# Linear attention's seams: two weight splits issued later, and three turned groups behind an output tile instead of two

## The chip, the cores and the metric

The kernel runs on one core of a Trainium2 chip. The metric is the device time of one execution in microseconds (us). The kernel before has a median of 2364.84 us over 3 runs (2358.07 to 2365.14). All other times come from one profiled execution, whose own time is 2364.55 us and whose span from first to last instruction is 2362.6 us.

## The reference, cut to what matters

Two layers of a first block (a projection, a spatial gating group and an attention group, an output projection) are followed by one layer of gated linear attention and a convolutional feed-forward part, all on 1024 tokens of width 1024 in fp32. What the change touches:

```python
# end of each layer of the first block: y = [y_a, y_b], 1024 wide
out = jnp.einsum('bse,ed->bsd', y, w_out[l])

# linear attention, per chunk of 64 tokens (4 heads, dk 128, dv 256)
q_dec, k_inv = qi * jnp.exp(bi), ki * jnp.exp(-bi)
scores = jnp.where(causal, einsum('bhtd,bhsd->bhts', q_dec, k_inv), 0.0)
o = einsum('bhts,bhsv->bhtv', scores, vi) + einsum('bhtd,bhdv->bhtv', q_dec, state)
state = state * exp(b_last) + einsum('bhsd,bhsv->bhdv', ki * exp(b_last - bi), vi)
# its end
return (rms_norm(o) * jax.nn.silu(r)) @ w_out
```

## The kernel before, in words

Every large product is made of three fp32r matmuls: both operands are split into a high part (`hi`) and a low part (`lo`), and `three_products` (lines 200 to 202) adds hi*hi, hi*lo and lo*hi into one PSUM bank. Weights come in pieces of 128x2048 by DMA into `w_raw` (two slots). ScalarE (ACT) writes `w_hi` (`split_hi`, line 168), VectorE (DVE) writes `w_lo` (`split_lo`, line 184). Each engine has a program written out by hand; its instructions run in that order and wait on semaphores. A load of piece u waits until the piece that held its slot has been split. A piece's first split waits until the matmuls that used its `w_hi` slot are done.

The left operand needs tokens in the free dimension, so activations are turned by TensorE (PE) transposes. `TurnHalf` turns one half of the width in eight groups of four 128x128 transposes: `pe` (line 229) writes a PSUM bank, `act` (line 235) takes it to `hT_hi`, `dve` (line 239) subtracts to get `hT_lo`. With `banks` banks, group g waits until group g - banks is through `dve`.

An output projection runs by `pe_wide_tile`: a tile is 128 tokens by 512 columns, half of the depth, 12 matmuls. In its first pass over eight tiles the first four tiles use banks 0 to 3, and behind each of them two groups of the second half are turned, into banks 4 to 7. Ahead of tile 4, PE waits for all eight groups. There are three such passes: in `MixerOut.pe_first` (called in `mixer_to_mixer` and in `mixer_to_gla`) and in `gla_out_ffn`.

The linear attention has three programs in a row in one block. `mixer_to_gla` ends with four pieces of columns for the queries and keys; behind each piece v, ACT and DVE split piece v + 2, the last one being the second piece of the core's gate weights. `gla_core` then waits for the last scaled keys (`heads_done`). For each of eight tiles of 128 tokens, PE computes scores in two parts (lines 1793 and 1797), the second from the mixed keys `KM` that ACT makes (`key_map`, lines 1897 and 1899); GpSimd (POOL) makes `KE` (line 1779), PE turns it (line 1807), ACT takes it to `KEt` (line 1910), and PE multiplies it with the values (line 1815). DVE masks the scores (line 1946) and updates the state (line 1952 for the first tile). Behind the core's tiles come the gate's products, ACT's `gate` (line 1921) and DVE's `gated` (line 1989), and, one group behind each tile, the turning of the first half of the output's width. `gla_out_ffn` starts its first pass when all eight of those groups are through DVE.

Of the kernel before, what the change touches and what calls it, by code (L numbers as in the profile page):

```python
# [16 lines left out]
TT = SEQ // P  # L17
# [190 lines left out]
class TurnHalf:  # L208
# [9 lines left out]

    def bank(self, g):
        return self.p.ps[:, self.bank0 + g % self.banks, :]  # L220

    def place(self, hT, g):
        return hT[:, self.k0 + g // 2, g % 2 * 512:(g % 2 + 1) * 512]
# [856 lines left out]
class MixerOut:  # L1080
# [51 lines left out]
    def pe_first(self, pe):  # L1132

        w = self.w
        for t in range(TT):
            if t == 4:
                pe.wait_ge(self.turn.lo_done, self.turn.GROUPS)
            mm = pe_wide_tile(self.p, 0, t, t, w.slot(0))
            if t < 4:
                self.turn.pe(pe, 2 * t, self.src)  # L1140
                self.turn.pe(pe, 2 * t + 1, self.src)
        mm.then_inc(self.half_done, 1)
        w.ready(pe, 1)
        for t in range(TT):
            pe_wide_tile(self.p, 1, t, t, w.slot(1)).then_inc(self.acc_ready, 1)
        w.ready(pe, 2)
        for t in range(TT):
            pe.wait_ge(self.acc_free, t + 1)
            mm = pe_wide_tile(self.p, 0, t, t, w.slot(2))
        mm.then_inc(self.half_done, 1)  # L1150
# [185 lines left out]
GLA_PIECES = 8  # L1336
# [24 lines left out]
def mixer_to_gla(prog, a, outs, ins, follows, src, x_src, x_dst):  # L1361
# [28 lines left out]
    U0 = OUT_PIECES  # L1390
# [12 lines left out]
    w = Weights(prog, pieces + [(follows, u) for u in range(2)], used, resident=1)  # L1403
# [168 lines left out]
    def act_program(act):  # L1572
        def square(act, t):
            act.wait_ge(out.x_done, t + 1)
            norm.square(act, t, ring.tile(t))

        def take(g, t, bank):
            act.wait_ge(acc_ready, g * TT + t + 1)
            nc.scalar.activation(V[:, t, g * WIDE:(g + 1) * WIDE], prog.ps[:, bank, :], ACT.Copy,
                                 scale=norm.inv(t)).then_inc(acc_free, 1)  # L1580

        out.act_first(act)
        for i in range(TT + TURN):
            if i == 0:
                w.split_hi(act, 4)
            at_tile(out.act_tile, act, i)
            at_tile(nxt.hi, act, i - TURN)
            at_tile(square, act, i - 2)
            if i == TT:
                w.split_hi(act, 5)  # L1590
        norm.root(act, 0)
        norm.root(act, 1)
        act.wait_ge(norm.inverted, 2)
        for t in range(4):
            take(0, t, V_TILES[t])
        w.split_hi(act, U0 + 2)
        act.wait_ge(wa_landed, 16)
        nc.scalar.activation(wa[:, :, 0, :], wa_raw[:], ACT.Copy).then_inc(wa_hi_done, 1)
        for t in range(4, TT):
            take(0, t, V_TILES[t])  # L1600
        act.wait_ge(scales_ready, 1)
        for half in range(2):
            nc.scalar.activation(scales[:, half * 512:(half + 1) * 512], prog.ps[:, 4 + half, :],
                                 ACT.Copy).then_inc(scales_taken, 1)
        w.split_hi(act, U0 + 3)
        act.wait_ge(small_landed, SMALL)
        for n in range(2 * GH):
            h, half = n // 2, n % 2
            act.wait_ge(z_ready, n + 1)
            if n >= 2:  # L1610
                act.wait_ge(z_exp, n - 1)
            nc.scalar.activation(tmp[:, n % 2, :], prog.ps[:, 4 + n % 4, :], ACT.Abs,
                                 bias=ba[:, h:h + 1]).then_inc(z_abs, 1)
            act.wait_ge(z_abs, n + 1)
            nc.scalar.activation(B[:, h, half * 512:(half + 1) * 512], tmp[:, n % 2, :], ACT.Exp,
                                 scale=-1.0).then_inc(z_exp, 1)
        act.wait_ge(z_exp, 2 * GH)
        for h in range(GH):
            nc.scalar.activation(B[:, h, :], B[:, h, :], ACT.Ln, bias=1.0).then_inc(z_log, 1)
        w.split_hi(act, U0 + 4)  # L1620
        for t in range(TT):
            take(1, t, t)
        w.split_hi(act, U0 + 5)
        for h in range(GH):
            act.wait_ge(b_done, h + 1)
            nc.scalar.activation(Q[:, h, :], B[:, h, :], ACT.Exp, scale=1.0 / TAU).then_inc(e_done, 1)
        nc.scalar.activation(DEC[:], Bv[:, :, :, CH - 1], ACT.Exp, scale=1.0 / TAU).then_inc(e_done, 1)
        act.wait_ge(e_done, GH + 1)
        for h in range(GH):
            nc.scalar.activation(B[:, h, :], B[:, h, :], ACT.Exp, scale=-1.0 / TAU).then_inc(e_done, 1)  # L1630
        for v in range(4, GLA_PIECES):
            w.split_hi(act, U0 + v + 2)

    def dve_program(dve):
# [46 lines left out]
        for v in range(4, GLA_PIECES):  # L1681
            for i in range(4):
                h, half = (v % 2) * 2 + i // 2, i % 2
                tok = slice(half * 512, (half + 1) * 512)
                dve.wait_ge(acc_ready, 2 * TT + 4 * (v - 4) + i + 1)
                if v < 6:
                    dve.wait_ge(q_scaled, h + 1)
                    nc.vector.scalar_tensor_tensor(Q[:, h, tok], prog.ps[:, i, :], DK ** -0.5, Q[:, h, tok],
                                                   ALU.mult, ALU.mult).then_inc(acc_free, 1)
                else:  # L1690
                    dve.wait_ge(k_scaled, h + 1)
                    nc.vector.tensor_tensor(K[:, h, tok], prog.ps[:, i, :], B[:, h, tok],
                                            ALU.mult).then_inc(acc_free, 1)
            w.split_lo(dve, U0 + v + 2)
    def heads_done(engine, heads=GH):

        engine.wait_ge(acc_free, 2 * TT + 8 + 2 * heads)
# [4 lines left out]
def gla_core(prog, a, into, stream, follows):  # L1702

    nc = prog.nc
    _, w_in, Q, K, V, DEC, norm, heads_done, k_scaled, z_ready = into
# [24 lines left out]
    w = Weights(prog, [(stream, u) for u in range(NU)] + [(follows, u) for u in range(2)], used, prior=w_in)  # L1730
# [22 lines left out]
    turn = TurnHalf(prog, 0, 0, 6)  # L1753
# [126 lines left out]
    def act_program(act):  # L1880
# [11 lines left out]
        def key_map(t):  # L1892
            if t >= 2:
                act.wait_ge(s_ready, t - 1)
                act.wait_ge(ke_done, t - 1)
            for h in range(GH):
                nc.scalar.activation(KM[:, t % 2, h, 0:CH], K[:, h, t * P:t * P + CH], ACT.Copy,
                                     scale=DEC[:, h, 2 * t:2 * t + 1])
            nc.scalar.activation(KM[:, t % 2, :, CH:P], K[:, :, t * P + CH:(t + 1) * P], ACT.Copy
                                 ).then_inc(km_done, 1)  # L1900

        heads_done(act)
        key_map(0)
        key_map(1)
        for t in range(TT):
            if t + 1 < TT:
                act.wait_ge(ke_turned, t + 1)
                if t >= 2:
                    act.wait_ge(kv_ready, t - 1)
                nc.scalar.activation(KEt[:, t % 2, :, :], prog.ps[:, 1, :].rearrange("p (h d) -> p h d", h=GH),  # L1910
                                     ACT.Copy).then_inc(ke_taken, 1)
            if t + 2 < TT:
                key_map(t + 2)
            if t >= 1:
                head_squares(t - 1)
# [13 lines left out]
        for i in range(TT + 2):  # L1929
            if i < TT:  # L1930
                gate(TT + i)
            if i >= 2:
                turn.act(act, i - 2)
            if i == TT - 1:
                w.split_hi(act, 5)

    def dve_program(dve):
        dve.wait_ge(zeroed, 2)
# [3 lines left out]
        def mask_scores(t):  # L1942
            dve.wait_ge(s_ready, t + 1)
            if t >= 2:
                dve.wait_ge(inter, t - 1)
            nc.vector.copy_predicated(S[:, t % 2, :, :], mask[:].unsqueeze(1).to_broadcast([P, GH, P]),
                                      prog.ps[:, 0, :].rearrange("p (h d) -> p h d", h=GH)).then_inc(s_done, 1)
# [28 lines left out]
                                               ALU.mult).then_inc(o_done, 1)  # L1976

        mask_scores(0)
        for t in range(TT):
            if t + 1 < TT:  # L1980
                state(t)
                mask_scores(t + 1)
            if t >= 1:
                normed(t - 1)
# [13 lines left out]
        for i in range(TT + 2):  # L1998
            if i < TT:
                gated(TT + i)  # L2000
            if i >= 2:
                turn.dve(dve, i - 2)
            if i == TT - 1:
                w.split_lo(dve, 5)

    def src(t, k):
        return V[:, t, k * P:(k + 1) * P]
# [34 lines left out]
def gla_out_ffn(prog, a, core, outs, ups, downs, x_src, x_dst, y_dst):  # L2042
# [129 lines left out]
    def pe_program(pe):  # L2172
# [7 lines left out]
        for t in range(TT):  # L2180
            if t == 4:
                pe.wait_ge(turn.lo_done, turn.GROUPS)
            mm = pe_wide_tile(prog, 0, t, t, w.slot(0))
            if t < 4:
                turn.pe(pe, 2 * t, src)
                turn.pe(pe, 2 * t + 1, src)
        mm.then_inc(o_half_done, 1)
        w.ready(pe, 1)
        for t in range(TT):
# [370 lines left out]
```

## Time and profile before

| what | value |
|---|---|
| median of 3 runs | 2364.84 us (2358.07 to 2365.14) |
| profiled execution | 2364.55 us, span 2362.6 us |
| PE busy | 2298.8 us, 97% of the span |
| VectorE busy | 1064.9 us, 45% |
| ScalarE busy | 895.5 us, 38% |
| GpSimd busy | 271.2 us, 11% |
| mean granted clock of PE | 0.990 |

PE is nearly always busy, so the time can be read as PE's busy time plus what PE waits. A row of the waits names the instruction that waited, the one that released it, the sum of the idle time, how often, and the longest. The granted clock is 1.00 at 2.4 GHz and 0.50 at 1.2 GHz.

### The profile page before, as it was taken

The page shows a single profiled execution, that of the slowest core. Times are in us where ns is not written, and L with a number is a line of the kernel's source. Part 1 is how long each engine was busy: PE and PEld are TensorE (multiplying, and loading weights), DVE is VectorE, ACT ScalarE, POOL GpSimd, SP SyncE. Part 2 cuts the span into 40 slices and gives each one's busy share as a digit, 9 for nine tenths or more (in the row PEclk, how much of TensorE's full clock was granted, in tenths as well). Part 3 has the DMA queues.
Part 4 walks back from the last instruction along what each step waited for, and adds up shares of the span by engine and source line. Part 5 has one row for each costly group of instructions (what it writes and reads, how often), then busy time and mean ns, then how long its engine had stood idle before and what let it go on. Part 6 is the DMA issues. An engine that isn't in the chain of part 4 may idle for free.

```text
span 2362.6 us, 28595 instructions
## 1 busy us (share of the span) xinstructions
PE 2298.8 (97%) x11648; PEld 1930.4 (82%) x11648; DVE 1064.9 (45%) x1433; ACT 895.5 (38%) x1420; POOL 271.2 (11%) x276
## 2 busy tenths in 40 slices
PE   7999999989999999999999999999999999999998
PEld 7887788878988778888878888787888888888887
DVE  4323388844433258882614243325433433443343
ACT  5122477733321268772434042213221222222242
POOL 0097200000029600000003020000000000000000
PEclk9999999999999999999999999999999999999999
DMA  5111000032311000004311100133111111114332
GB/s 197 36 54 36 1 1 1 1 134 104 101 47 54 18 1 1 1 1 143 141 40 36 63 19 22 59 109 107 52 38 53 53 36 53 53 61 162 107 124 72
DMA packets 104050, 141.34 MB, mean 60 GB/s; under 512 B 11574, under 2 KB 64998, under 8 KB 103942
## 3 DMA queue, kind: packets, MB, share of 16 engines
q1 hardware_dynamic: 103942, 139.84, 17.9%
q8 instruction: 76, 1.25, 0.2%
q14 instruction: 32, 0.26, 0.0%
HBM read 123.05 MB, written 16.78 MB: 59 GB/s over the span
## 4 chain that ended last, share of the span: by engine, by line
PE 51%; DVE 2%; ACT 1%; issue 0%; POOL 0%; DVEq 0%; ACTq 0%
PE ps L200 16%; PE ps L202 16%; PE ps L201 16%; PE ps L1815 1%; PE ps L1828 1%; PE ps L1837 1%; DVE hT_lo L291 0%; PE ps L229 0%; PE ps L1500 0%; ACT w_hi L168 0%; DVE w_lo L184 0%; PE ps L1793 0%; PE ps L1797 0%; PE ps L276 0%; DVE OUT L2432 0%
## 5 line engine op out<-in xcount | busy, mean ns | idle before, releaser
L200 PE MATMUL ps<-w_hi,hT_hi 128*128 128x512 f32 (+1 forms) x1760 | 683.2, 388 | 16.7 <-DVE hT_lo L239 10.0
L202 PE MATMUL ps<-w_hi,hT_lo 128*128 128x512 f32 (+1 forms) x1760 | 675.9, 384 | 0.0
L201 PE MATMUL ps<-w_lo,hT_hi 128*128 128x512 f32 (+1 forms) x1760 | 675.6, 384 | 0.0
L184 DVE TENSOR_TENSOR w_lo<-w_raw,w_hi 128x2048 fp32r<-128x2048 f32 x90 | 207.8, 2309 | 547.6 <-ACT w_hi L168 545.1
L200 PEld LDWEIGHTS ps<-w_hi,hT_hi 128*128 128x128 f32 x1760 | 334.1, 190 | 84.1 <-issue 14.3
L202 PEld LDWEIGHTS ps<-w_hi,hT_lo 128*128 128x128 f32 x1760 | 333.7, 190 | 65.3
L201 PEld LDWEIGHTS ps<-w_lo,hT_hi 128*128 128x128 f32 x1760 | 334.4, 190 | 63.0 <-issue 0.5
L168 ACT ACTIVATE w_hi<-w_raw 128x2048 fp32r<-128x2048 f32 x72 | 137.7, 1913 | 522.2 <-PE ps L202 522.2
L200 PE MATMUL ps<-hT_hi,w_hi 128*128 128x512 f32 x832 | 325.9, 392 | 5.1 <-DVE X L2372 2.8
L201 PE MATMUL ps<-hT_lo,w_hi 128*128 128x512 f32 x832 | 325.4, 391 | 0.0
L202 PE MATMUL ps<-hT_hi,w_lo 128*128 128x512 f32 x832 | 325.4, 391 | 0.0
L200 PEld LDWEIGHTS ps<-hT_hi,w_hi 128*128 128x128 f32 x832 | 157.3, 189 | 38.2 <-issue 3.0
L201 PEld LDWEIGHTS ps<-hT_lo,w_hi 128*128 128x128 f32 x832 | 157.3, 189 | 32.9
L202 PEld LDWEIGHTS ps<-hT_hi,w_lo 128*128 128x128 f32 x832 | 157.2, 189 | 32.8
L1048 DVE TENSOR_REDUCE nmx<-ps 128x1 f32<-128x1024 f32 x128 | 155.7, 1218 | 59.5 <-PE ps L878 59.5
L1061 DVE TENSOR_TENSOR PT_lo<-ps,PT_hi 128x512 fp32r<-128x512 f32 x256 | 163.7, 681 | 1.1 <-ACT PT_hi L975 1.1
L975 ACT ACTIVATE PT_hi<-ps 128x512 fp32r<-128x512 f32 x256 | 139.2, 595 | 63.4 <-PE ps L890 59.1
L981 ACT ACTIVATE PR<-ps,nmx 128x1024 f32<-128x1024 f32 x128 | 142.9, 1116 | 15.0 <-DVE nmx L1048 13.9
L890 PEld LDWEIGHTS ps<-ident,PR 128*128 128x128 f32 x1024 | 114.9, 140 | 38.7 <-issue 21.8
L890 PE MATMUL ps<-ident,PR 128*128 128x128 f32 x1024 | 138.0, 276 | 6.8 <-DVE PT_lo L1061 5.2
L2409 DVE SCALAR_TENSOR_TENSOR A<-ps,CW,A 128x1023 f32 (+3 forms) x44 | 56.4, 1283 | 175.1 <-ACT A L2324 171.0
L904 PE MATMUL ps<-PT_hi,VS 128*128 128x256 f32 x512 | 130.4, 293 | 1.4 <-DVE PT_lo L1061 1.4
(191 smaller groups left out, 2367.3 us busy)
## 6 DMA issues: line engine op xcount, KB each, us to landing
w_raw<-in_w_in SPq DMA_DIRECT2D x22, 1024.0 KB, 5.1
w_raw<-in_ffn_w_up SPq DMA_DIRECT2D x44, 512.0 KB, 4.8
w_raw<-in_ffn_w_down SPq DMA_DIRECT2D x22, 1024.0 KB, 4.9
x_mid<-X SPq DMA_DIRECT2D x24, 512.0 KB, 2.8
w_raw<-in_gla_w_in SPq DMA_DIRECT2D x12, 1024.0 KB, 5.2
X<-in_x SPq DMA_DIRECT2D x16, 512.0 KB, 6.9
w_raw<-in_w_out SPq DMA_DIRECT2D x8, 1024.0 KB, 6.7
X<-x_mid SPq DMA_DIRECT2D x16, 512.0 KB, 7.3
```

The source lines that it names most:

```text
L168: self.p.nc.scalar.activation(self.p.w_hi[:, slot, 0:stream.size], self.p.w_raw[:, slot, 0:stream.size], ACT.Copy).then_inc(self.hi_ready, 1)
L184: engine.tensor_tensor(self.p.w_lo[:, slot, 0:size], self.p.w_raw[:, slot, 0:size], plane(self.p.w_hi[:, slot, 0:size]), ALU.subtract).the ...
L200: nc.tensor.matmul(out, a_hi, b_hi, start=first, stop=False)
L201: nc.tensor.matmul(out, a_hi, b_lo, start=False, stop=False)
L202: return nc.tensor.matmul(out, a_lo, b_hi, start=False, stop=last)
L890: mm = nc.tensor.transpose(prog.ps[:, 4 + half, j * P:(j + 1) * P], self.PR[m % 3][:, k * P:(k + 1) * P], prog.ident[:])
L904: nc.tensor.matmul(prog.ps[:, 7, 0:256], v, self.PT_hi[:, g % 2, k, :], start=(k == 0), stop=False)
L975: nc.scalar.activation(self.pt_of(self.PT_hi, m, half), self.bank_of(half), ACT.Copy).then_inc(self.pt_hi, 1)
L981: nc.scalar.activation(self.PR[n % 3][:].rearrange("p (a b) -> p a b", a=2), prog.ps[:, 2 * (n % 2):2 * (n % 2) + 2, :], ACT.Exp, bias=sel ...
L1048: nc.vector.tensor_reduce(self.nmx[:, n:n + 1], prog.ps[:, 2 * (n % 2):2 * (n % 2) + 2, :], AX.XY, ALU.max, negate=True).then_inc(self.max ...
L1061: nc.vector.tensor_tensor(self.pt_of(self.PT_lo, m, half), self.bank_of(half), plane(self.pt_of(self.PT_hi, m, half)), ALU.subtract).then_ ...
L2409: nc.vector.scalar_tensor_tensor(o, banks(j, part)[:, 0:SEQ - back].unsqueeze(1), CW[:, 2 - back, bass.ds(f, 1)], o, ALU.mult, ALU.add).th ...
```

## The change

There are three edits. The core's last weight split of `mixer_to_gla` is issued by `gla_core` instead: on ACT behind the mixed keys of tiles 0 and 1, on DVE behind the first masked scores. The split of the last piece of the core (the second of the output's weights) is issued behind the last turned groups, not ahead of them. In the three first passes three groups are turned behind tiles 0 and 1 and two behind tile 2, where two were turned behind each of tiles 0 to 3.

```diff
@@ TurnHalf
+    def behind(self, t):
+        return range(3 * t, min(3 * t + 3, self.GROUPS))
@@ MixerOut.pe_first, and the same in gla_out_ffn
-            if t < 4:
-                self.turn.pe(pe, 2 * t, self.src)
-                self.turn.pe(pe, 2 * t + 1, self.src)
+            for g in self.turn.behind(t):
+                self.turn.pe(pe, g, self.src)
@@ mixer_to_gla, act_program
-        for v in range(4, GLA_PIECES):
+        for v in range(4, GLA_PIECES - 1):
             w.split_hi(act, U0 + v + 2)
@@ mixer_to_gla, dve_program
-            w.split_lo(dve, U0 + v + 2)
+            if v < GLA_PIECES - 1:
+                w.split_lo(dve, U0 + v + 2)
@@ gla_core, act_program
         key_map(0)
         key_map(1)
+        w_in.split_hi(act, len(w_in.pieces) - 1)
@@ gla_core, act_program
             if i >= 2:
                 turn.act(act, i - 2)
-            if i == TT - 1:
-                w.split_hi(act, 5)
+        w.split_hi(act, 5)
@@ gla_core, dve_program
         mask_scores(0)
+        w_in.split_lo(dve, len(w_in.pieces) - 1)
@@ gla_core, dve_program
             if i >= 2:
                 turn.dve(dve, i - 2)
-            if i == TT - 1:
-                w.split_lo(dve, 5)
+        w.split_lo(dve, 5)
```

## Rows read from the trace of the kernel before

**Rows 1.** The page: the engines' busy time, and the chain that ended last.

```profile
PE 2298.8 (97%) x11648; PEld 1930.4 (82%) x11648; DVE 1064.9 (45%) x1433; ACT 895.5 (38%) x1420; POOL 271.2 (11%) x276
PE 51%; DVE 2%; ACT 1%; issue 0%; POOL 0%; DVEq 0%; ACTq 0%
```

**Rows 2.** Waits of PE, whole span: who waited for whom, us, times, longest.

```profile
PE ps L200 <- DVE hT_lo L239: 10.0, 4, 5.3
PE ps L1797 <- ACT KM L1899: 1.4, 1, 1.4
PE ps L1815 <- ACT KEt L1910: 0.7, 1, 0.7
```

**Rows 3.** Timeline of a first pass: start, us, engine, line, count, [idle before].

```profile
506.25 0.39 PE L202 MATMUL ps<-w_hi,hT_lo 128*128 128x512 f32 x1
...
508.53 1.04 PE L229 MATMUL ps<-ident,G 128*128 128x128 f32 x8
509.17 1.08 ACT L235 ACTIVATE hT_hi<-ps 128x512 fp32r<-128x512 f32 x2 [2.53 <-PE ps L229]
509.80 1.29 DVE L239 TENSOR_TENSOR hT_lo<-ps,hT_hi 128x512 fp32r<-128x512 f32 x2 [2.33 <-ACT hT_hi L235]
511.14 0.50 PE L200 MATMUL ps<-w_hi,hT_hi 128*128 128x512 f32 x1 [1.58 <-DVE hT_lo L239]
...
1530.09 1.03 PE L229 MATMUL ps<-ident,V 128*128 128x128 f32 x8
1533.71 1.04 PE L229 MATMUL ps<-ident,V 128*128 128x128 f32 x8
```

**Rows 4.** Timeline of the core's end, PE, ACT and DVE.

```profile
1515.19 1.47 PE L229 MATMUL ps<-ident,V 128*128 128x128 f32 x12
1515.97 0.59 ACT L235 ACTIVATE hT_hi<-ps 128x512 fp32r<-128x512 f32 x1
1516.45 1.91 ACT L168 ACTIVATE w_hi<-w_raw 128x2048 fp32r<-128x2048 f32 x1
1516.71 0.68 DVE L239 TENSOR_TENSOR hT_lo<-ps,hT_hi 128x512 fp32r<-128x512 f32 x1
1518.39 2.29 DVE L184 TENSOR_TENSOR w_lo<-w_raw,w_hi 128x2048 fp32r<-128x2048 f32 x1 [0.99 <-ACT w_hi L168]
1520.60 1.28 DVE L239 TENSOR_TENSOR hT_lo<-ps,hT_hi 128x512 fp32r<-128x512 f32 x2
1521.98 0.77 PE L200 MATMUL ps<-w_hi,hT_hi 128*128 128x512 f32 x1 [5.32 <-DVE hT_lo L239]
```

**Rows 5.** Timeline of the core's start, all engines.

```profile
1363.35 1.91 ACT L168 ACTIVATE w_hi<-w_raw 128x2048 fp32r<-128x2048 f32 x1 [19.84 <-PE ps L202]
1365.17 1.05 ACT L1897 ACTIVATE KM<-Kd,DEC 128x64 f32<-128x64 f32 x4
1366.58 1.10 PE L1797 MATMUL ps<-Qd,KM 128*128 128x64 f32 x8 [1.43 <-ACT KM L1899]
1366.60 1.89 POOL L1779 TENSOR_TENSOR KE<-KM,DEC 128x512 f32<-128x512 f32 x1 [1.78 <-ACT KM L1899]
1367.38 0.40 ACT L1899 ACTIVATE KM<-Kd 128x256 f32<-128x256 f32 x1
1369.70 0.60 ACT L1910 ACTIVATE KEt<-ps 128x512 f32<-128x512 f32 x1 [1.91 <-PE ps L1807]
1370.35 3.78 PE L1815 MATMUL ps<-V,KEt 128*128 128x256 f32 x8 [0.69 <-ACT KEt L1910]
1374.23 1.22 DVE L1952 COPY ST<-ps 128x1024 f32<-128x1024 f32 x1 [5.69 <-PE ps L1815]
1378.51 1.89 PE L1815 MATMUL ps<-V,KEt 128*128 128x256 f32 x8
```

**Rows 6.** Stretches: length, busy time of PE, PEld, DVE, ACT, POOL, granted clock, DMA.

```profile
1536.00:1542.00 6.00, 4.43 (x24) 3.51 (x23) 1.55 (x3) 1.08 (x2) 0.00 (x0) 1.00 0.39 154
1364.00:1377.00 13.00, 9.98 (x49) 8.56 (x50) 4.70 (x4) 5.66 (x18) 4.06 (x6) 0.74 0.24 81
1518.00:1526.00 8.00, 4.02 (x11) 3.19 (x12) 3.49 (x3) 1.33 (x3) 0.00 (x0) 0.57 0.51 181
1156.00:1161.00 5.00, 4.15 (x16) 3.65 (x17) 4.86 (x9) 2.29 (x5) 0.00 (x0) 0.66 1.01 407
```

**Rows 7.** Timeline: a shorter wait, and the next splits of both GLA stages.

```profile
1156.85 1.91 PE L276 MATMUL ps<-ident,H 128*128 128x128 f32 x8 [1.90 <-DVE hT_lo L291]
1447.75 1.92 ACT L168 ACTIVATE w_hi<-w_raw 128x2048 fp32r<-128x2048 f32 x1 [19.40 <-PE ps L202]
1551.27 1.92 ACT L168 ACTIVATE w_hi<-w_raw 128x2048 fp32r<-128x2048 f32 x1 [12.20 <-PE ps L202]
```

More of the change, by code:

```diff
@@ L2183, in pe_program @@
             mm = pe_wide_tile(prog, 0, t, t, w.slot(0))
-            if t < 4:
-                turn.pe(pe, 2 * t, src)
-                turn.pe(pe, 2 * t + 1, src)
+            for g in turn.behind(t):
+                turn.pe(pe, g, src)
         mm.then_inc(o_half_done, 1)
```

## Prediction

> **What bounds the kernel.** I read the page first: PE is busy for 97% of the span, no other engine for half of it [rows 1]. So a change pays only where it shortens a wait of PE or raises PE's clock. The view of PE's waits is second: three of its rows lie where the change is. PE waited 10.0 us in four places for the low parts of turned groups, once for 5.3 us; the linear attention's start cost it 1.4 us for the mixed keys and 0.7 us for the turned keys [rows 2]. The timelines around these places come third, and a view of stretches fourth, for the granted clock.
>
> **Three groups behind a tile, in three passes.** Before: eight transposes start at 508.53, ACT's first copy at 509.17, DVE's first subtraction at 509.80, DVE is through at 511.09, and PE, which waits for all eight groups, restarts at 511.14 after 1.58 us idle [rows 3]. The 10.0 us less the 5.3 us leave 4.7 us for three passes, 1.57 us each [rows 2]. Ten matmuls go from 506.25 to 508.53, 0.228 us each, so a tile of 12 takes 2.74 us; from one pair of groups to the next it is 1533.71 - 1530.09 = 3.62 us, so two groups take 0.88 us [rows 3].
>
> After: groups 6 and 7 are turned behind tile 2, and tile 3 stands between them and the wait. Their low parts are ready 511.09 - 508.53 = 2.56 us after their first transpose; PE reaches tile 4 after 0.88 + 2.74 = 3.62 us. The wait goes, with 1.06 us to spare. The number of transposes and matmuls is the same. The new wait is that for a bank: groups 4 and 5, behind tile 1, need groups 0 and 1 through DVE, and groups 6 and 7 need 2 and 3. DVE takes about 0.61 us a group (1.29 for two that overlap by 0.07), so three groups are through 1.27 + 3 x 0.61 + 0.07 = 3.17 us after the first transpose; PE needs 1.32 + 2.74 = 4.06 us until it asks for the first of them again. No wait. SP issues the loads that stand behind the last group's transposes (gain, rows of X) some 4 us earlier; PE waits for none of them in the view of waits, so I give nothing for that. **4.7 us gained**, bounds 4.4 to 4.7.
>
> **The core's end.** Before: the last 12 transposes start at 1515.19 and end at 1516.66. ACT copies group 5 and then splits a piece (1516.45, 1.91 us) before groups 6 and 7; DVE subtracts group 5 at 1516.71, then splits (1518.39, 2.29 us), then subtracts the last two at 1520.60 until 1521.88; PE restarts at 1521.98 [rows 4]. After: ACT copies group 6 at 1516.45 and 7 at about 1516.94, until 1517.5; DVE follows group 5 with 6 and 7 at 0.61 us steps and is through at 1516.71 + 2 x 0.61 + 0.68 = 1518.61. PE restarts at 1518.71. **3.27 us gained**, bounds 3.1 to 3.4; 2.05 us of wait stay. The split now runs from 1517.4 to 1519.3 on ACT and to about 1521.7 on DVE. Behind it on both queues stand the first groups of the next stage, turned not before 1518.71 + 2.74 = 1521.45 plus a copy, so DVE is just free. The piece is used a whole pass (over 25 us) later. SP's load that waits for this low part slips by 1 us, to 1521.7; its slot is split next after 1551.27 [rows 7]. Hidden.
>
> **The core's start.** Before: ACT splits from 1363.35, makes the first mixed keys from 1365.17; PE's second scores start at 1366.58, KE at 1366.60 on POOL for 1.89 us, KEt at 1369.70, the product L1815 at 1370.35 [rows 5]. After: ACT can start the mixed keys when the last scaled keys are there (PE's L1793 started on them at 1364.04). Two of them take 1367.38 - 1365.17 + 0.40 = 2.61 us, the first about 1.35. So second scores and KE start at 1365.45, 1.13 us earlier. The split, 1.91 us, stands behind both: from 1366.6 to 1368.5. The turned keys are in PSUM by 1365.5 + 1.89 + 0.6 = 1368.0 at the latest, but KEt is queued behind the split: it starts at 1368.4, ends at 1369.0, and L1815 starts at 1369.04. So 1.31 us of the seam goes, and what is late next is the moved split itself: PE waits 1 to 1.8 us for KEt, where it waited 0.7. On DVE the split runs 1368.5 to 1370.8, and behind it stands the state copy L1952, which waits for L1815's result; that took from 1370.35 to 1374.13 with PE at half clock and would take 1.89 at full [rows 5], so it comes at 1370.9 at the earliest. Just hidden. SP's next load slips 3 us, its slot is split next at 1447.75 [rows 7]. **1.3 us gained**, bounds 0.9 (KE and KEt as before plus a lost overlap) to 1.8.
>
> Sum: 4.7 + 3.3 + 1.3 = 9.3 us, from 2364.55 to 2355.25.
>
> **The clock.** Both GLA seams cost PE its clock: 0.74 over 1364 to 1377 and 0.57 over 1518 to 1526, and in both PE had been mostly idle before it fell from 2.4 to 1.2 GHz [rows 6]. At the core's start L1815 took 3.78 us instead of 1.89 [rows 5]; 0.26 x 13 / 0.5 = 6.8 us ran at half clock, of which about 5.2 was work of PE behind L1815's start, so 2.6 us were lost there. At the end 0.43 x 8 / 0.5 = 6.9 us, 3.8 us of it behind the restart at 1521.98: 1.9 us lost. After the change 2 us of idle stay at each. A wait as short as 1.90 us was followed by 0.66 over 5 us [rows 6, 7], while the 1.57 us of a first pass kept 1.00 [rows 6]. So it is open which way 2 us go: credit 0 to 4.5 us, or a loss of 1.6 if a later fall now lies wholly on dense matmuls. Nearest is the row of 1.90 us, whose fall was half as long (0.34 x 5 / 0.5 = 3.4 us). I take 1.5 us. That gives 2353.8.
>
> The Trainium skill, "TensorE: Matmul & The Clock Gate", section "Why this matters for your kernels", would keep the full clock through idle gaps of this length: it has only clearly longer ones give it up. By that page the sum would be 2355.25 - 4.5 = 2350.7, and the fall behind 1.90 us speaks against it. It is the second case below.
>
> **Cases.** One: as summed, clock still lost at one or both seams, for less long: 2353.8, range 2351.8 to 2356. Chance 0.52. For it: every step is read off queues of which the order is fixed.
>
> Two: the clock stays at 2.4 GHz at both seams: 2350.7. For it the 1.57 us waits, against it the 1.90 us one. Chance 0.16.
>
> Three: the waits go, but the clock is lost as long as before, or one more stretch falls on dense matmuls elsewhere; 6.8 us at half clock cost 3.4: 2355.3 to 2358.7, say 2357. For it: the same kernel ran at 2358.07 and at 2365.14, more than its waits can explain. Chance 0.20.
>
> Four: the core's start gains nothing, since KEt behind the split takes the wait over and DVE's split then holds the state copy: 2356.5. Against it: both have their place in the sums above. Chance 0.08.
>
> Five, the other side: the change moves all work behind 511 by 1.6 us and more, and PE's other short waits (the 1.90 us one, [rows 7]) then fall so that the clock drops at more of them, twice as long. Each such stretch of 6.8 us costs 3.4; from three more on, 10.2 us exceed the 9.3: 2365.5 or more. Against it: fewer and shorter waits should give fewer falls. Chance 0.04.
>
> **Range.** 2349.8 to 2358.5: it takes the first two cases and most of the third and fourth. What a measurement of this kernel can tell from no change is about 0.3%, 7.1 us. A gain over 7.1 us, below 2357.7, comes in the first two cases, half of the third and most of the fourth, less for a median that stands 7 us above its lowest run: 0.75. Within 0.3%: 0.22. Slower by more: 0.03. The profiled time is 0.3 us below the median, so the sum needs no shift.
>
> **What would show it.** The waits of PE for L239 fall from four (10.0 us) to one of about 2.0 us. The wait of L1797 for KM falls to about 0.3 us, that of L1815 for KEt grows to 1 to 1.8 us, and ACT's L168 stands between L1899 and L1910. If a row of L229 waiting for L239 appears, the bank step is wrong; if L1952 starts right behind L184 with PE waiting, the DVE step is. The granted clock around both seams decides between the cases.

## The result, and the profile after

The changed kernel ran at a median of 2347.5 us (2342.27 to 2349.78, 6 runs), the kernel before at 2363.56 us (2357.99 to 2366.9, 6 runs): ratio 0.9937, 95% interval 0.9924 to 0.995. In a second comparison it was 2345.76 us, ratio 0.9928 (0.9913 to 0.9944). The forecast was 2353.8, with 2349.8 as the lower end of its range. The direction was right and the size was short: some 16 us where 11 were forecast.

The page of the changed kernel, first line and the line of the engines' busy time:

```profile
span 2343.3 us, 28595 instructions
PE 2288.4 (98%) x11648; PEld 1922.4 (82%) x11648; DVE 1064.4 (45%) x1433; ACT 895.6 (38%) x1420; POOL 270.5 (12%) x276
```

The span fell by 19.3 us. PE ran the same 11648 matmuls in 10.4 us less (2298.8 before, [rows 1]), and idled 8.9 us less (2362.6 - 2298.8 = 63.8 us before, 2343.3 - 2288.4 = 54.9 us after). The second part is the waits. The first is mostly the clock, as no matmul was removed. Not all of it is the edit's: in the kernel before the clock fell to half at 491.29 us, ahead of the first instruction that the edit moves, and in this trace it did not. The section on the experiments takes the two apart.

The waits of PE in the changed kernel (who waited for whom, us, times, longest):

```profile
PE ps L200 <- DVE hT_lo L243: 2.0, 1, 2.0
PE ps L1819 <- ACT KEt L1915: 1.8, 1, 1.8
PE ps L1801 <- ACT KM L1903: 0.3, 1, 0.3
```

These answer to [rows 2]: 10.0 us in four places became 2.0 in one, 1.4 became 0.3, and 0.7 became 1.8, as forecast. The timeline of both seams (start, us, engine, line, [idle before]), to be laid beside [rows 4, 5]:

```profile
1355.11 1.06 ACT L1901 ACTIVATE KM<-Kd,DEC 128x64 f32<-128x64 f32 x4 [20.51 <-DVE Kd L1695]
1356.53 1.10 PE L1801 MATMUL ps<-Qd,KM 128*128 128x64 f32 x8 [0.30 <-ACT KM L1903]
1357.64 1.89 ACT L168 ACTIVATE w_hi<-w_raw 128x2048 fp32r<-128x2048 f32 x1
1359.44 0.57 ACT L1915 ACTIVATE KEt<-ps 128x512 f32<-128x512 f32 x1
1360.07 3.37 PE L1819 MATMUL ps<-V,KEt 128*128 128x256 f32 x8 [1.76 <-ACT KEt L1915]
...
1504.68 1.56 ACT L239 ACTIVATE hT_hi<-ps 128x512 fp32r<-128x512 f32 x3
1505.42 1.88 DVE L243 TENSOR_TENSOR hT_lo<-ps,hT_hi 128x512 fp32r<-128x512 f32 x3
1507.40 0.47 PE L200 MATMUL ps<-w_hi,hT_hi 128*128 128x512 f32 x1 [2.04 <-DVE hT_lo L243]
1510.23 1.48 PE L233 MATMUL ps<-ident,V 128*128 128x128 f32 x12
1514.32 1.48 PE L233 MATMUL ps<-ident,V 128*128 128x128 f32 x12
```

The split (L168) stands between the mixed keys and KEt and holds KEt back; at the core's end ACT and DVE take groups 5, 6 and 7 in one go; the first pass turns three groups (12 transposes) behind a tile, with no wait for a bank. Now the clock, in stretches of the changed kernel (length, busy time of PE, PEld, DVE, ACT, POOL, granted clock, DMA share, GB/s):

```profile
1352.00:1365.00 13.00, 10.14 (x55) 8.30 (x54) 4.95 (x4) 6.17 (x17) 2.81 (x5) 0.87 0.14 42
1502.00:1515.00 13.00, 10.96 (x64) 9.21 (x64) 7.57 (x10) 5.63 (x10) 0.00 (x0) 1.00 0.26 90
1147.00:1165.00 18.00, 16.08 (x86) 13.07 (x85) 17.55 (x28) 11.25 (x22) 0.00 (x0) 1.00 0.55 221
```

Over the core's start the clock is 0.87 where it was 0.74 over as many us [rows 6], over the core's end 1.00 where eight us had 0.57. The third row is a place that no edit touches, the second mixer's wait of 1.90 us [rows 7]. The same stretch of the kernel before:

```profile
1147.00:1165.00 18.00, 16.10 (x78) 13.30 (x77) 17.41 (x27) 9.31 (x23) 0.00 (x0) 0.91 0.80 290
```

PE is busy equally long, but it ran part of that at 1.2 GHz: 78 matmuls against 86. (The work of the changed kernel is 7.7 us ahead there, so the two rows hold the same wait but not quite the same matmuls.)

### The profile page after: what moved, and what is told of

Its sections match the earlier page's. It is cut to its first block, busy times and chain, and to the rows that moved or that the text cites. A ratio compares the mean times of both kernels' runs of the same rounds, so it can differ in the third digit from the quotient of the medians.

```text
span 2343.3 us, 28595 instructions
## 1 busy us (share of the span) xinstructions
PE 2288.4 (98%) x11648; PEld 1922.4 (82%) x11648; DVE 1064.4 (45%) x1433; ACT 895.6 (38%) x1420; POOL 270.5 (12%) x276
## 4 chain that ended last, share of the span: by engine, by line
PE 52%; DVE 2%; ACT 1%; issue 0%; DVEq 0%; ACTq 0%
PE ps L200 16%; PE ps L202 16%; PE ps L201 16%; PE ps L1832 1%; PE ps L1819 1%; PE ps L1841 1%; DVE hT_lo L295 0%; PE ps L233 0%; PE ps L1503 0%; PE ps L1801 0%; PE ps L1797 0%; PE ps L280 0%; DVE w_lo L184 0%; DVE X L1220 0%; DVE OUT L2435 0%
## 5 line engine op out<-in xcount | busy, mean ns | idle before, releaser
L168 ACT ACTIVATE w_hi<-w_raw 128x2048 fp32r<-128x2048 f32 x72 | 137.8, 1913 | 504.8 <-PE ps L202 504.8
```

What stands on the lines that cost most here:

```text
L168: self.p.nc.scalar.activation(self.p.w_hi[:, slot, 0:stream.size], self.p.w_raw[:, slot, 0:stream.size], ACT.Copy).then_inc(self.hi_ready, 1)
```

## The experiments

Times differ by up to 12 us between executions of one kernel, so each comparison is a ratio to the kernel before, run beside it on the same chip. One us is 0.0004 of it.

**The parts alone, and the kernel before again.** e1_tiles has only the third edit, e2_end only the second, e3_start only the first; e4_before has none.

```diff
# e1_tiles: of the change, only
+            for g in self.turn.behind(t):
+                self.turn.pe(pe, g, self.src)
# e2_end: of the change, only (and the same for DVE)
-            if i == TT - 1:
-                w.split_hi(act, 5)
+        w.split_hi(act, 5)
# e3_start: of the change, only (and the same for DVE)
+        w_in.split_hi(act, len(w_in.pieces) - 1)
```

Expected of e1_tiles: 

> The kernel before with the first passes alone changed (three turned groups behind a tile). Theory A (each removed wait also gives back clock that it cost in part of the executions): the three waits of 1.57 us go, 4.7 us, and the mean granted clock rises a little, so 5 to 7 us faster. Theory B (waits alone; what the change gained above 9.3 us is the chance of where the clock falls): 4.7 us faster, mean granted clock as in the kernel before.

Expected of e2_end: 

> The kernel before with the core's last weight split alone moved behind the last turned groups. The wait for L239 of 5.3 us falls to 2.0 us: 3.3 us. Theory A: the fall of the clock behind it goes or halves, so 4.5 to 6.5 us faster. Theory B: 3.3 us faster, the same 6.8 us at 1.2 GHz somewhere around the restart.

Expected of e3_start: 

> The kernel before with the split at the core's start alone moved behind the mixed keys. L1815 starts 1.3 us earlier relative to the last scaled keys. Theory A: the stretch at 1.2 GHz there halves from 6.8 to 3.4 us, 2.5 to 3.5 us faster in all. Theory B: 1.3 us faster, the stretch stays 6.8 us long.

Expected of e4_before: 

> The kernel before, unchanged, to see how much its stretches at 1.2 GHz differ between executions. Theory A: the falls at the two GLA seams are there again, 6.8 us each, and others come and go. Theory B: the falls at the seams come and go as well, and the time follows the mean granted clock by chance alone. Both: ratio 1.00 to the kernel before within 0.3%.

Measured: e1_tiles 0.9971 (0.996 to 0.9983), e2_end 0.9981 (0.9969 to 0.9992), e3_start 1.0002 (0.9994 to 1.0011), e4_before 0.9995 (0.9984 to 1.0006). In us of 2362: 6.9, 4.5, -0.5. The first two lie in the ranges of theory A, but their intervals (4.0 to 9.4 and 1.9 to 7.3 us) hold theory B too. In e4_before both seams have their 6.8 us at 1.2 GHz again, as its theory A says, and other falls differ. e3_start fits neither theory: its waits are 0.3 and 1.8 us as in the changed kernel, yet nothing is gained. Its trace shows why:

```profile
1363.00:1381.00 18.00, 15.92 (x75) 14.09 (x75) 5.91 (x7) 10.51 (x32) 4.45 (x7) 0.72 0.18 59
```

There are 0.28 x 18 / 0.5 = 10 us at 1.2 GHz at the core's start, where the kernel before had 6.8 and the changed kernel, with the same instructions there, 0.13 x 13 / 0.5 = 3.4. And the three parts add up to 10.9 us, not 16.

**The changed kernel again, and three variants of it or of before.** e6_fill_end_before keeps the wait at the core's end and has PE busy in it. e7_after_fill does that for both seams of the changed kernel. e8_late moves the split one step on.

```diff
# e6_fill_end_before, on the kernel before, behind the core's last turned group
+        pe.wait_ge(turn.lo_done, 4)
+        w.ready(pe, 4)
+        for n in range(22):
+            nc.tensor.matmul(prog.ps[:, 3, :], prog.hT_hi[:, 4 + n % 4, 0:P], prog.w_hi[:, w.slot(4), 0:WIDE],
+                             start=True, stop=True)
# e7_after_fill, on the changed kernel: the same with 8, and behind turn_keys(0)
+        w.ready(pe, 0)
+        for n in range(7):
+            nc.tensor.matmul(prog.ps[:, 7, :], prog.hT_hi[:, n % 4, 0:P], prog.w_hi[:, w.slot(0), 0:WIDE],
+                             start=True, stop=True)
# e8_late, on the changed kernel (on DVE likewise, behind state(0))
         key_map(1)
-        w_in.split_hi(act, len(w_in.pieces) - 1)
@@ behind the first copy to KEt
+            if t == 0:
+                w_in.split_hi(act, len(w_in.pieces) - 1)
```

Expected of e5_after (the changed kernel): 

> The changed kernel again, unchanged, for more executions and a second trace. Theory A (the waits give 9 us, the clock gives 4 to 6 us more, every time): 13 to 16 us faster than before, both seams with at most 3.4 us at 1.2 GHz each. Theory B (the surplus in the first result was chance): about 9.3 us faster, and the second trace has stretches at 1.2 GHz as long as those of the kernel before.

Expected of e6_fill_end_before: 

> The kernel before; during the wait of 5.3 us at the core's end PE runs 22 matmuls (128x512, 0.23 us each, 5.0 us) into a PSUM bank that nothing reads, so the wait for L239 is the same but PE isn't idle in it. Nothing else changes. Theory A (the idle wait costs the clock, and the clock costs 1.8 us or more behind it): the granted clock is 1.00 over the seam and the kernel is 1.5 to 4 us faster though it does more work. Theory B (the clock falls for other reasons there): no change, or slower by what the matmuls overrun.

Expected of e7_after_fill: 

> The changed kernel with 7 such matmuls in the wait for KEt at the core's start (1.8 us) and 8 in the wait at the core's end (2.0 us). Theory A: what the clock still costs at the two seams goes, 0.5 to 3 us faster than the changed kernel, 14 to 18 us faster than before. Theory B: equal to the changed kernel within 1 us.

Expected of e8_late: 

> The changed kernel with the moved split behind the first KEt on ACT, and behind the first state copy on DVE, in place of behind the mixed keys. The wait of L1815's products for KEt falls from 1.8 to about 0.6 us: 1.2 us faster than the changed kernel by the waits, 1 to 3 us with the clock (theory A), 1.2 us or less (theory B). If the split on DVE then holds the second masked scores, the wait comes back at the scores' product instead and nothing is gained.

Measured: e5_after 0.9928 (0.9913 to 0.9944), 17.0 us, so it is no chance that the change gains more than 9.3 us. e6_fill_end_before 0.9987 (0.9977 to 0.9998): 3 us faster (0.5 to 5.4) with 22 matmuls more. Its timeline and its stretch over the seam:

```profile
1515.36 5.28 PE L1882 MATMUL ps<-w_hi,hT_hi 128*128 128x512 f32 x22
1520.93 0.47 PE L200 MATMUL ps<-w_hi,hT_hi 128*128 128x512 f32 x1 [0.29 <-issue]
```

```profile
1512.00:1524.00 12.00, 11.71 (x59) 9.46 (x59) 5.92 (x7) 4.26 (x6) 0.00 (x0) 1.00 0.28 87
```

The tile starts as late as before after the transposes, but the clock is 1.00, also over the eight us (1518 to 1526) where it was 0.57. So idle time of 5.3 us does cost the clock there. What that is worth can be read from the traces more closely than from the 3 us: from this tile's first product to the first transposes of the next stage (at 1610.38 in the kernel before, 1607.66 here) it is 1610.38 - 1521.98 = 88.40 us before and 1607.66 - 1520.93 = 86.73 us here, 1.7 us less for the same work. The forecast had 1.9.

e7_after_fill has 1.00 over both seams too, and 0.9925 (0.9909 to 0.994): no better than the changed kernel within the intervals. e8_late has 0.9921 (0.9906 to 0.9937); its timeline:

```profile
1363.82 1.90 ACT L168 ACTIVATE w_hi<-w_raw 128x2048 fp32r<-128x2048 f32 x1
1363.97 3.39 PE L1819 MATMUL ps<-V,KEt 128*128 128x256 f32 x8 [0.69 <-ACT KEt L1914]
1368.61 2.28 DVE L184 TENSOR_TENSOR w_lo<-w_raw,w_hi 128x2048 fp32r<-128x2048 f32 x1
1370.81 0.74 DVE L1951 COPY_PREDICATED S<-mask,ps 128x512 f32<-128x512 uint32 x1
```

The wait for KEt is back at 0.69 us, and PE had no other wait in its place. That is 1.1 us less idle time, too little to tell from the changed kernel. Neither run decides between its theories.

**All pairs of parts.** Together with the parts alone and the whole this makes eight kernels, with and without each part.

```diff
# e9_tiles_end: the change without
+        w_in.split_hi(act, len(w_in.pieces) - 1)
# e10_tiles_start: the change without
+        w.split_hi(act, 5)
# e11_end_start: the change without
+            for g in self.turn.behind(t):
# e12_late_fill: e8_late, and behind the core's last turned group
+        for n in range(8):
+            nc.tensor.matmul(prog.ps[:, 3, :], prog.hT_hi[:, 4 + n % 4, 0:P], prog.w_hi[:, w.slot(4), 0:WIDE],
+                             start=True, stop=True)
```

Expected of e9_tiles_end: 

> The kernel before with the three first passes and the core's end changed, the core's start as before. The parts alone gave 0.29% (passes), 0.19% (core's end) and nothing (core's start), together less than the 0.63 to 0.72% of the whole change. Theory A (waits 8.0 us, clock at the core's end and at the passes, and the parts simply add): 0.48%, 11.3 us faster. Theory C (the parts do not add, since the clock at one place depends on what went before): more than 13 us faster, and near the whole change.

Expected of e10_tiles_start: 

> The first passes and the core's start changed, the core's end as before. Theory A: 0.29% and nothing, 6.8 us faster, with a stretch of 6.8 to 10.2 us at 1.2 GHz at the core's start as in the start edit alone. Theory C: 9 us or more faster, the stretch at the core's start 3.4 us as in the whole change.

Expected of e11_end_start: 

> The core's end and start changed, the first passes as before. Theory A: 0.19% and nothing, 4.5 us faster. Theory C: 7 us or more faster.

Expected of e12_late_fill: 

> The version that the runs point to: the changed kernel, its split at the core's start behind the first KEt, and 8 matmuls (128x512, read by nothing) in the wait of 2.0 us at the core's end. Theory A: 1.2 us by the wait for KEt and up to 1 us by the clock faster than the changed kernel, 0.73 to 0.8% faster than before. Against it: at the core's end the clock was 1.00 in both traces of the changed kernel, so the matmuls there have nothing to give back and can only overrun.

| kernel | ratio | us faster, of 2362 | by its waits |
|---|---|---|---|
| passes (e1) | 0.9971 | 6.9 | 4.7 |
| end (e2) | 0.9981 | 4.5 | 3.3 |
| start (e3) | 1.0002 | -0.5 | 1.3 |
| passes, end (e9) | 0.9949 (0.9932 to 0.9965) | 12.0 | 8.0 |
| passes, start (e10) | 0.9966 (0.9954 to 0.9977) | 8.0 | 6.0 |
| end, start (e11) | 0.9968 (0.9959 to 0.9978) | 7.6 | 4.6 |
| all (two comparisons) | 0.9937, 0.9928 | 15.9 | 9.3 |

Each part's worth is the mean over the four pairs of kernels that differ by it alone. Passes: 6.9, 7.5, 8.5, 8.3, mean 7.8 us. End: 4.5, 5.1, 8.1, 7.9, mean 6.4. Start: -0.5, 1.1, 3.1, 3.9, mean 1.9. Each of these differences is uncertain by 2 to 5 us either way. e9 and e10 lie between their theories A and C and e11 at C, so that the parts fail to add is indicated, not shown. e12_late_fill, at 0.9937 (0.9921 to 0.9953), is no better than the changed kernel: its matmuls at the core's end gave nothing back, since the clock stayed there anyway. No version tried beats the changed kernel beyond the intervals; e8_late has the least idle time.

**The same work in every trace.** The times above carry the chance of where the clock falls in each execution. The traces can be compared without it, by the time from the start of one of PE's instructions to that of another, where no fall lies between, or the same one, or only the one that is to be priced. For the second of the three passes the two are these, first in the kernel before ([rows 7] has the second), then in the changed kernel:

```profile
1063.08 0.47 PE L200 MATMUL ps<-w_hi,hT_hi 128*128 128x512 f32 x1 [3.06 <-PEq L90]
1057.26 0.47 PE L200 MATMUL ps<-w_hi,hT_hi 128*128 128x512 f32 x1 [3.06 <-PEq L90]
1149.15 1.16 PE L280 MATMUL ps<-ident,H 128*128 128x128 f32 x8 [1.89 <-DVE hT_lo L295]
```

| stretch of PE's work | as before, us | with the edit, us | gain |
|---|---|---|---|
| second pass, between the rows above | 93.77 (e11: 93.78) | 91.89 (e9, e10: 91.91) | 1.9 |
| third pass, from the tile behind the core's end to the next stage's transposes | 86.77 (e2), 86.78 (e11) | 84.85 (e9: 84.83) | 1.9 |
| second mixer, from its wait of 1.90 us to the first L1500 (L1503 after) | 68.71 | 67.48 | 1.2 |
| core's start, from the first scores to the last second scores | 54.60 | 52.18 to 52.45 | 2.3 |
| core's end, from there to the tile behind it | 103.34 | 100.06 to 100.10 | 3.3 |
| clock behind the core's end, with the third pass as before | 88.40 | 86.77 (e2), 86.73 (e6) | 1.6 |

The first pass gives 1.9 as well. From the product behind the wait of 2.99 us that ends at 491.96 in the kernel before to the transposes behind the next wait of 1.90 us it is 96.67 us there and 94.74 in e10, both with 6.8 us at 1.2 GHz on the way, and 93.81 (e3) and 91.93 (changed kernel) where neither has them. So the change's own places give 3 x 1.9 + 1.2 + 2.3 + 3.3 + 1.6 = 14.1 us; the mean of the two comparisons, 15.9, holds that within its interval. In the one pair of profiles it is 19.3 us, and some 4 us of the difference lie ahead of the first moved instruction: the fall at 491.29, worth 96.67 - 93.81 = 2.9 us, and 1.0 us before it. There is a fall at this untouched wait in 10 of the 16 traces, with the passes as before and with them changed, so as far as the edit goes it is chance. Behind the waits of 2.8 and 1.9 us near 1625 and 1645 the traces with three groups behind a tile lose 1.5 us less on average, but the two sets overlap, so that this belongs to the edit is not shown.

A pass gives 1.9 us although its idle row was 1.57. The row counts from the modelled end of the last transposes, while a product that need not wait starts before that end:

```profile
504.92 1.03 PE L229 MATMUL ps<-ident,G 128*128 128x128 f32 x8
505.70 0.48 PE L200 MATMUL ps<-w_hi,hT_hi 128*128 128x512 f32 x1
```

Without a wait the product starts 0.78 us after the transposes, with it 511.14 - 508.53 = 2.61 us after [rows 3]: the stall was 1.83 us.

**Why do the passes give still more?** In none of the traces does the clock fall behind a pass's own wait of 1.57 us. It falls, or not, at the untouched wait near 1155. The stretch 1147 to 1165 had 0.91 in five of the six traces with two groups behind a tile (the profile of before, e3, e4, e6, e11; not e2) and 1.00 in all eight with three (after, e1, e5, e7 to e10, e12). Two of them, e11 first, then e9:

```profile
1147.00:1165.00 18.00, 16.10 (x79) 13.37 (x78) 17.41 (x27) 9.29 (x22) 0.00 (x0) 0.91 0.81 291
```

```profile
1147.00:1165.00 18.00, 16.10 (x84) 13.13 (x82) 17.45 (x28) 10.99 (x24) 0.00 (x0) 1.00 0.64 247
```

Two runs put PE work in place of the old wait, so that the timing of before is restored without its idle time:

```diff
# e13_pad, on the changed kernel, in all three passes; e14_pad_gla: only in mixer_to_gla
                 pe.wait_ge(self.turn.lo_done, self.turn.GROUPS)
+                for n in range(7):
+                    self.p.nc.tensor.matmul(self.p.ps[:, 4, :], self.p.hT_hi[:, n % 4, 0:P],
+                                            self.p.w_hi[:, w.slot(0), 0:WIDE], start=True, stop=True)
```

Expected of e13_pad: 

> The changed kernel with 7 matmuls (128x512, 1.6 us, read by nothing) ahead of tile 4 in each of the three first passes, where PE used to wait 1.57 us. Their work costs 3 x 1.6 = 4.8 us. Theory I (idle time in the pass cost the clock later): the clock stays 1.00 at the wait of 1.90 us near 1155, and the kernel is 4.8 us slower than the changed one, 10.5 to 11 us faster than before. Theory T (timing): the clock falls there again as in the kernel before, and the kernel is 6 to 8.5 us slower than the changed one, equal to the version with the passes left as before (e11, 0.9968).

Expected of e14_pad_gla: 

> The same 7 matmuls only in the pass of the stage from mixer to linear attention. Theory I: no fall near 1155, 1.6 us slower than the changed kernel. Theory T: the fall of 3.4 us near 1155 is back, and the kernel is 2.5 to 4 us slower than the changed one.

Measured: e13_pad 0.9959 (0.9944 to 0.9973), 6.3 us behind the changed kernel's mean of 0.99325, where its work is 4.8. e14_pad_gla 0.9945 (0.9928 to 0.9962), 3.0 us behind, where its work is 1.6. Both times are those of theory T, but the intervals hold theory I too. The stretches, e13_pad first, then e14_pad_gla with its core's start:

```profile
1147.00:1165.00 18.00, 16.10 (x77) 13.12 (x76) 17.41 (x27) 9.22 (x22) 0.00 (x0) 0.91 0.80 292
```

```profile
1147.00:1165.00 18.00, 16.10 (x87) 13.32 (x86) 17.45 (x28) 10.36 (x24) 0.00 (x0) 1.00 0.72 265
1356.00:1372.00 16.00, 13.35 (x58) 11.72 (x59) 5.50 (x5) 8.23 (x24) 4.47 (x7) 0.68 0.20 67
```

In e13_pad the fall is back though PE no longer idles in the pass, as timing wants it and idle time does not. In e14_pad_gla it is not, against theory T; there the clock was lost for 0.32 x 16 / 0.5 = 10 us at the core's start instead, where all instructions are those of the changed kernel. Nor did e2_end have the fall, with its passes as before. With one trace each, this leans to timing and doesn't settle it.

## Why the prediction missed

**The passes, by their waits: the mechanism right, the price short.** All three waits of 1.57 us went, no wait for a bank came, and tile 4 found its groups done. But 4.7 us was the sum of the idle rows; the stalls were 1.83 us each by [rows 3] and the row at 505.70, and the same work takes 1.9 us less per pass, 5.7 in all.

**The core's end, by its wait: right.** 3.27 us forecast; the wait fell from 5.32 to 2.04 us, and DVE's three groups ended at 1505.42 + 1.88 = 1507.30, 0.1 us ahead of the restart.

**The core's start: right.** The second scores wait 0.30 us, KEt stands behind the split, and L1819 starts 1.76 us after the turned keys. From the first scores (1364.04 before, 1355.13 after) to this product it is now 4.94 us where it was 6.31: 1.37 us, with 1.31 forecast. DVE's split was done at 1361.86, ahead of the state copy. POOL's KE took 1.05 us where the forecast had kept 1.89 (the last section has the reason as far as it is seen); it was not on the path, since KEt waited for the split.

**The sum of the waits: right as idle time.** 9.3 us forecast, 8.9 us less idle time in the profile; the transposes of the keys, at full clock in the new trace, are the other 0.5 us that stood in L1815's start. As time between the same instructions it is 5.7 + 3.3 + 1.4 = 10.4 us.

**The clock: this step failed.** The forecast took 1.5 us as the credit, at the two GLA seams only. By the same work in the traces the clock gave 1.6 us behind the core's end, 0.9 us at the core's start (2.3 less the 1.4 of its waits) and 1.2 us behind the wait near 1155: 3.7 us. With the 1.0 us that the passes' price was short, that is 14.1 us where 10.8 were forecast. The mean measured gain is 15.9; the 1.8 us between lie within the interval, and no run assigns them. (By the mean worth of each part less its wait, in the table of pairs, the clock's shares would be 3.1 us at the core's end, 0.6 at its start and 3.1 for the passes, each uncertain by some us.) Two things were mis-sized.

First, at the core's end the forecast allowed the fall to stay, as one had followed a wait of 1.90 us elsewhere [rows 6, 7]. It does not: the clock fell there in all 5 traces with the idle wait of 5.32 us (before, e1, e3, e4, e10), in none of the 8 with 2.04 us of idle time (the changed kernel twice, e2, e8, e9, e11, e13, e14), and in none of the 3 with matmuls in the wait. Case two had the size right, 1.9 us for 1.6 to 1.7 measured, and too small a chance.

Second, the passes got no credit because their own waits had kept 1.00 [rows 6]. That row is right, and it was the wrong place to look. What such an edit changes is also when the later short waits come, and the one near 1155 stopped costing the clock. The fifth case had this mechanism, as a risk only, and with the sign against the change; the third took falls elsewhere as chance. For this stretch chance is a poor account: 5 of 6 traces against 0 of 8. For the falls behind the waits near 489 and 1060 it is the better one, since they come and go on both sides of the edit.

By the Trainium skill, "TensorE: Matmul & The Clock Gate", section "Why this matters for your kernels", idle gaps as short as those left keep the full clock. At the core's end the traces of the changed kernel agree, 1.00 behind 2.04 us. At its start they do not: 0.87 with no gap above 1.76 us. The sum by that page, 2350.7, would still have been 4 us above the mean of the two medians, 2346.6, since it looks at the two seams alone. Nor does the wait near 1155 agree, whose 1.90 us were followed by a fall in 5 of 6 traces.

Open: why the stretch at 1.2 GHz at the core's start, 6.8 us in all 6 traces with the start as before, has two lengths with the start edit and the same instructions. It was 3.4 us in e10, e11, e13 and both traces of the changed kernel, where the seam gains some 2.3 us, and 10 us in e3 and e14, which lose 0.7 and 0.6 us. That is why the start edit gained nothing alone. In e3 and e14 the fall began 0.9 and 1.3 us ahead of the values' product (L1819 in the changed kernel), in the other five 0.1 to 0.6 us ahead of it; that this decides the length was not tried by itself. Open too: what makes the clock fall, or not, behind the wait near 1155.

## What to carry to other kernels

Where PE is busy for 97% of the time, price each wait twice: the stall, which can be read off the queues to a tenth of a us, and the half clock that may follow, which was worth about 4 us beside 10 here. Measure the stall from start to start, against a place where the same product need not wait; the idle row was 0.3 us short of it. Look for the second price also at short waits that the edit does not touch: one of them stopped costing the clock here when its work came some us earlier. One profile shows one draw, so take several, and compare the time between the same two instructions before crediting a difference to the edit. If a wait can't be shortened, matmuls that nobody reads keep the clock through it, but they pay only where the clock does fall.

## What the hardware showed unexpectedly

PE can lose its clock while it is busy. In the kernel before, from 1227 to 1247 us, PE has no wait and 20.00 us of busy time:

```profile
1227.00:1247.00 20.00, 20.00 (x54) 12.69 (x53) 8.49 (x10) 13.65 (x20) 0.00 (x0) 0.74 0.17 52
```

The groups of the same stretch (busy us, mean ns):

```profile
L200 PE MATMUL ps<-w_hi,hT_hi 128*128 128x512 f32 x14 | 7.6, 541 | 0.0
L1500 PE MATMUL ps<-AL,wau 32*128 32x512 f32 x14 | 7.0, 637 | 0.0
```

A quarter of the matmuls there are products with a contraction of 32 rows. Each of the 16 traces has falls in this work, 3.4 to 10.2 us in all, whatever the edit. That the small contraction is the reason was not tried.

GpSimd's first KE takes 1.89 us in the six traces where VectorE's split runs beside it, and 1.05 us in the ten where it does not. The split in the kernel before (its KE is in [rows 5]), and the first KE of the changed kernel:

```profile
1365.30 2.29 DVE L184 TENSOR_TENSOR w_lo<-w_raw,w_hi 128x2048 fp32r<-128x2048 f32 x1 [1.31 <-ACT w_hi L168]
1356.55 1.05 POOL L1783 TENSOR_TENSOR KE<-KM,DEC 128x512 f32<-128x512 f32 x1 [0.64 <-ACT KM L1903]
```

Moving the split away shortened it by 0.84 us, which nothing waited for here.
